# Turning the experts' inner rows in two row tiles of 64 tokens, in a decoder stack on one NeuronCore

## Chip, cores and metric

The kernel runs on one NeuronCore of a Trainium2 chip. The time is device microseconds of one execution; a figure for a kernel is the median of several runs. Engines: PE is TensorE's matmul, PEld its weight load, DVE VectorE, ACT ScalarE, POOL GpSimd, SP the engine that issues the weight transfers.

## What is computed

Two decoder blocks on 256 tokens of width 1024, all in fp32, end in a mixture of experts, in which this change lies. Cut to that part:

```python
def swiglu(h, wg, wu, wd):
    return (jax.nn.silu(h @ wg) * (h @ wu)) @ wd

def moe_swiglu(h, router, wg, wu, wd):          # 8 experts, top 2, inner width 3584
    t = h.reshape(B * S, D)
    logits = t.astype(jnp.float32) @ router.astype(jnp.float32)
    top_v, top_i = lax.top_k(logits, TOP_K)
    top_w = jax.nn.softmax(top_v, axis=-1)
    gates = jnp.sum(jax.nn.one_hot(top_i, N_EXPERTS, dtype=jnp.float32) * top_w[..., None], axis=1)
    out = jnp.zeros_like(t)
    for e in range(N_EXPERTS):
        out = out + gates[:, e:e + 1].astype(t.dtype) * swiglu(t, wg[e], wu[e], wd[e])
    return out.reshape(B, S, D)
```

The products keep fp32 accuracy. Most of them are three matmuls of operands that were split into a high part and a low part (`mm3`, L567 to L569: high by high, low by high, high by low); some take fp32 as it is.

## The kernel before

The program first runs the dense layers (to about 880 us), then routes the tokens, and then `mixture` computes the experts. The eight experts are sorted by how many tokens chose them. The five fullest (j below 5, "wide" here) get places for 128 tokens, the three emptiest (j from 5 on, "narrow") places for 64. Tokens beyond the places go through a second pass, `experts(Again)`, behind a flag; it does not run with these inputs.

**Chunks.** An expert's inner width of 3584 is cut into 7 chunks of 512 columns. The list `order` gives the 56 chunks, 35 wide and 21 narrow, in the order B B B F B B F B B F B B F B F B B F B B F B F B B F B B F B F B B F B B F B F B B F B B F B F B B F B B F B F F, where B is wide and F narrow. Each chunk c reads 6 weight slabs of 1 MB: two for the gate rows, two for the up rows, two for the way down.

**One turn of the loop over c on PE** is written out by hand:

1. the gate rows of chunk c (`rows_by`, two slabs): 24 matmuls of 512 columns for a wide chunk (L567 to L569), 32 records of L1233 for a narrow one. A narrow matmul uses 64 columns of the array, with its two halves side by side, and takes fp32 as it is;
2. `turn_hidden(c - 1)`: the inner rows `hh` of the chunk before, 128 places by 512 numbers, are transposed on PE by L1212 (`e.transpose`, a matmul of 128 rows with the unit matrix in `cb`) into one PSUM bank. There are 4 transposes of 128 by 128 for a wide chunk and 2 for a narrow one, whose 64 places by 512 lie as 128 by 256;
3. the up rows of chunk c, as in 1;
4. the way down of chunk c - 1 (`down_by`, two slabs), which has the turned rows as its stationary operand: L567 to L569 with `hTH` and `hTL` (wide), L1266 with `hTS` (narrow);
5. now and then gathers of later tokens (L1168, L1181) or the scatter of a finished expert back to its tokens (L1195, L1196 wide; L1203 narrow, a matmul on 64 rows of the array, its two halves on rows 0 to 63 and 64 to 127, into two banks).

The turn of c - 1 stands between two sets of rows of chunk c. What surrounds it is therefore told by the kind of c, and how long it is by the kind of c - 1. The turns of chunks 0 to 54 stand so; that of 55 stands between the two slabs of chunk 54's way down, which is narrow.

**Banks.** Banks 0 to 2 hold the sums of the way down. Banks 3 to 7 are handed out in a ring (`Ring.take`) to gate rows, up rows, turns, gathers and scatters. `claim` makes PE wait until the bank's last reader is through.

**The other engines.** ACT (`hi_to`, L1461) rounds each wide slab of 128 by 2048 to its high part `splitH`, and DVE (`lo_to`, L2161) subtracts for the low part `splitL`, two slabs ahead of PE, into three buffers each. Between these ACT copies the turned rows out of the bank (`turned_hidden`, L1461 again: to `hTH` for a wide chunk, to `hTS` for a narrow one) and DVE subtracts for `hTL` (L2879, wide alone). ACT also takes silu of the gate rows (L1986), and DVE multiplies it with the up rows into `hh` (L2912). SP issues each slab's transfer as soon as its buffer is free. The semaphores of a turn are `S.h` (rows ready), `S.h_turn` (turned), `S.ht_hi` (copied by ACT) and `S.ht_lo` (low part by DVE).

Of the kernel before, what the change touches and what calls it, by code (L numbers as in the profile page):

```python
# [7 lines left out]
F = mybir.dt.float32  # L8
# [143 lines left out]
def program(nc, x, mem, consts, w, out, cap):  # L152
    ctx = ExitStack()
    with ctx:
# [347 lines left out]

        class Again:

            jobs, c0, lo0, pair0, scat0, add0, y0 = 3, 56, 35, 3, 32, 32, 10
            chunks = [(j, i) for j in range(3) for i in range(7)]
            pairs = [[0, 1], [2]]

# [23 lines left out]
        INV = 1.0 / 384  # L532
        CW = PCOL["conv_w"]
        mid_order = {(q, m): 2 * q + m for q in range(2) for m in range(2)}

        def pcol(name, i):
            c = PCOL[name] + i
# [16 lines left out]
        def tensor(e):  # L554
# [579 lines left out]
            def mixture():  # L1134
# [69 lines left out]
                                 start=True, stop=True).then_inc(S.scat, 1)  # L1204

                def turn_hidden(q):
                    j = order[q][0]
                    b = bank["h", q] = ring.take()
                    t.wait_ge(S.h, q + 1)
                    o = claim(b, (S.ht_lo, many[q] + 1) if j < 5 else (S.ht_hi, q + 1))  # L1210
                    for k in range(4 if j < 5 else 2):
                        mm = e.transpose(o[:, 128 * k:128 * k + 128], every_other(hh[q % 2], k), ident)  # L1212
                    mm.then_inc(S.h_turn, 1)

                def rows_by(n, o, j, s):

# [20 lines left out]
                def down_by(n, q, s):  # L1237

                    j, i = order[q]
                    if j < 5:  # L1240
                        H, Lo = pieces(n)
                        turns = [(k, half) for k in range(2) for half in range(2)]
                        if (i, s) == (6, 1):
                            turns = [(k, half) for half in range(2) for k in range(2)]
                        t.wait_ge(S.lo, cut(n))
                        t.wait_ge(S.ht_lo, many[q] + 1)
                        if (i, s) == (0, 0):
                            for half in range(2):
                                claim(half, (S.ye_lo, 2 * j + half + 1))
                        for k, half in turns:  # L1250
                            kk = 2 * s + k
                            mm = mm3(banks[half][:, :], hTH[q % 2][:, 128 * kk:128 * kk + 128],
                                     hTL[q % 2][:, 128 * kk:128 * kk + 128], H[:, k, 512 * half:512 * half + 512],
                                     Lo[:, k, 512 * half:512 * half + 512], (i, s, k) == (0, 0, 0),
                                     (i, s, k) == (6, 1, 1))
                            if (k, half) == turns[-1] or ((i, s) == (6, 1) and (k, half) == turns[1]):
                                mm.then_inc(S.prod, 1)
                    else:
                        V = whole(n)
                        t.wait_ge(landed[home[n]], filled[n])  # L1260
                        t.wait_ge(S.ht_hi, q + 1)
                        if (i, s) == (0, 0):
                            claim(2, (S.ys, j - 4))
                        for k in range(2):
                            for half in range(2):
                                mm = e.matmul(banks[2][64 * half:64 * half + 64, :],  # L1266
                                              hTS[q % 2][:, 128 * k + 64 * s:128 * k + 64 * s + 64],
                                              V[:, k, 512 * half:512 * half + 512], start=(i, s, k) == (0, 0, 0),
                                              stop=(i, s, k) == (6, 1, 1))
                        mm.then_inc(S.prod, 1)  # L1270
# [180 lines left out]
        def scalar(e):  # L1451
# [468 lines left out]
            def mixture():  # L1920
# [33 lines left out]
                                   gcol[:, k:k + 1])  # L1954

                def turned_hidden(q):
                    a.wait_ge(S.h_turn, q + 1)
                    if q > 1:
                        a.wait_ge(S.prod, prod(slab_of(q - 2, 5)))
                    if order[q][0] < 5:  # L1960
                        copy(hTH[q % 2][:, :], banks[bank["h", q]][:, :]).then_inc(S.ht_hi, 1)
                    else:
                        copy(hTS[q % 2][:, :], banks[bank["h", q]][:, 0:256]).then_inc(S.ht_hi, 1)

                for n in range(4):
                    evict(0, n)
# [63 lines left out]
            def experts(B):  # L2030
# [14 lines left out]
                                       gcol[:, k:k + 1])  # L2045

                def turned_hidden(q):
                    a.wait_ge(S.h_turn, B.c0 + q + 1)
                    if q > 1:
                        a.wait_ge(S.prod, prod(B.slab(q - 2, 5)))  # L2050
                    copy(hTH[q % 2][:, :], banks[bank["h again", q]][:, :]).then_inc(S.ht_hi, 1)
# [84 lines left out]
        def vector(e):  # L2136
# [699 lines left out]
            def mixture():  # L2836
# [38 lines left out]

                def turned_hidden(q):
                    if order[q][0] < 5:
                        v.wait_ge(S.ht_hi, q + 1)
                        e.tensor_tensor(hTL[q % 2][:, :], banks[bank["h", q]][:, :], hTH[q % 2][:, :].bitcast(F),  # L2879
                                        ALU.subtract).then_inc(S.ht_lo, 1)  # L2880

                v.wait_ge(S.route, 4)
                v.wait_ge(S.in_rt, 32)
# [11 lines left out]
                for c in range(len(order) + 1):  # L2895
                    held = []
                    if c < len(order):
                        j, i = order[c]
                        width = 512 if j < 5 else 256
                        for s in range(2):  # L2900
                            lo_to(min(slab_of(c, s) + 2, main_end - 1))
                        if j >= 5:
                            lo_to(min(slab_of(c, 2) + 2, main_end - 1))
                        if c > 0:
                            turned_hidden(c - 1)
                        for s in range(2, 4):
                            lo_to(min(slab_of(c, s) + 2, main_end - 1))
                        v.wait_ge(S.silu, c + 1)
                        v.wait_ge(S.prod, prod(slab_of(c, 3)))
                        if c > 1:  # L2910
                            v.wait_ge(S.h_turn, c - 1)
                        e.tensor_tensor(hh[c % 2][:, 0:width], sg[c % 2][:, 0:width],  # L2912
                                        banks[bank["gu", c, 1]][:, 0:width], ALU.mult).then_inc(S.h, 1)
                        if c == 0:
                            pick(0, False)
                            pick_few(True)
                        if c == 3:
                            pick_few(False)
                        if j in (0, 2):
                            p = j // 2 + 1  # L2920
                            if i == 1:
                                pick(p, True)
                            if 2 <= i <= 5:
                                held.append((p, i - 2))
                            if i == 6:
                                pick(p, False)
                        if c == 7:
                            v.wait_ge(S.flag, 2)
                            flags["dve"] = e.value_load(flag[0:1, 0:1], min_val=0, max_val=1)
                    if c > 0:  # L2930
                        j, i = order[c - 1]
                        n = slab_of(c - 1, 5)
                        for s in range(2):
                            lo_to(min(n + 1 + s, main_end - 1))
                            for p, nn in held[:1 - s]:
                                evict(p, nn)
                            for j_, tb, half in back.get((c, s), ()):
                                v.wait_ge(S.scat, back_no[j_, tb, half])
                                add_block(j_, tb, half)
                            if s == 0 and c == len(order) - 1:  # L2940
                                turned_hidden(c)
                        if i == 6 and j < 5:
                            for half in range(2):
                                o = slice(512 * half, 512 * half + 512)
                                v.wait_ge(S.ye_hi, 2 * j + half + 1)
                                split_cols(S.ye_lo, yL[:, o], yH[:, o], banks[half][:, :])
# [6 lines left out]
            def experts(B):  # L2953
# [24 lines left out]
                                           ALU.add).then_inc(S.moe_add, 1)  # L2978

                def turned_hidden(q):  # L2980
                    v.wait_ge(S.ht_hi, B.c0 + q + 1)
                    e.tensor_tensor(hTL[q % 2][:, :], banks[bank["h again", q]][:, :], hTH[q % 2][:, :].bitcast(F),
                                    ALU.subtract).then_inc(S.ht_lo, 1)

# [4 lines left out]
                for c in range(len(B.chunks) + 1):  # L2989
                    evicted = None  # L2990
                    if c < len(B.chunks):
# [7 lines left out]
                        v.wait_ge(S.silu, B.c0 + c + 1)  # L2999
                        v.wait_ge(S.prod, prod(B.slab(c, 3)))  # L3000
                        if c > 1:
                            v.wait_ge(S.h_turn, B.c0 + c - 1)
                        e.tensor_tensor(hh[c % 2][:, :], sg[c % 2][:, :], banks[bank["gu again", c, 1]][:, :], ALU.mult)\
                            .then_inc(S.h, 1)
                        p = j // 2 + 1
# [268 lines left out]
```

## Time and profile before

| | us |
|---|---|
| runs | 1779.03 to 1779.14, median 1779.09 (3 runs) |
| the profiled execution, its own time | 1782.06 |
| its span (first to last instruction) | 1780.2 |
| PE busy | 1736.2 (98%) |
| DVE busy | 1186.6 (67%) |
| ACT busy | 915.4 (51%) |
| transfers from HBM | 492.36 MB |

Durations are from the one profiled execution. A row of the timeline gives the start of the first instruction in it, the time to the end of the last, engine, line, operation, output and inputs, shape and count. The shape begins with the rows and columns of the array that are in use: 128\*64 is a matmul on 128 rows and 64 columns, 64\*128 one on 64 rows. Durations of PE and PEld overlap, since matmuls are pipelined; what one costs is read from start to start. "(x n)" or "xn" is the number of instructions. A wait names the one that waits, then the one waited for.

### The profile page before, as it was taken

What the parts mean: (1) busy time and instruction counts of PE and PEld (TensorE: products, weight loads), DVE (VectorE), ACT (ScalarE), POOL (GpSimd) and SP (SyncE); (2) the same over time, 40 slices, a digit from 0 to 9 for tenths busy, and PEclk for the clock granted to TensorE, in tenths of its full rate; (3) what the DMA queues carried; (4) which work ended last, traced back from release to release, by engine and by line L of the source; (5) the groups of instructions that cost most, each with busy time, mean ns of one, the idle gap of its engine ahead of it and who ended that gap; (6) DMA issues with size and microseconds to landing.
All of it is one profiled execution on the core that took longest, in us unless ns stands there. A gap on an engine that the chain in (4) does not pass through costs nothing.

```text
span 1780.2 us, 25131 instructions
## 1 busy us (share of the span) xinstructions
PE 1736.2 (98%) x10391; PEld 1426.0 (80%) x10391; DVE 1186.6 (67%) x1517; ACT 915.4 (51%) x992; POOL 55.5 (3%) x71
## 2 busy tenths in 40 slices
PE   7999998999999999999999999999999999999997
PEld 7988887899988899999787777777777777776774
DVE  5664666767689566569686677565765676675663
ACT  5345565555454434444475555554554555554542
POOL 0000000000060000032000000000000000000000
PEclk9999999999999999999999999999999999999999
DMA  9533442475544385555747999999999999999995
GB/s 319 165 95 120 142 166 95 151 259 183 175 140 143 117 256 169 186 144 193 278 167 310 390 394 394 422 420 421 414 369 386 422 407 418 414 403 415 418 418 227
DMA packets 157545, 495.13 MB, mean 278 GB/s; under 512 B 9609, under 2 KB 99439, under 8 KB 114415
## 3 DMA queue, kind: packets, MB, share of 16 engines
q1 hardware_dynamic: 152911, 489.04, 72.0%
q10 hardware_dynamic: 4512, 4.40, 0.9%
q8 instruction: 84, 1.38, 0.3%
q14 instruction: 38, 0.31, 0.0%
HBM read 492.36 MB, written 1.05 MB: 277 GB/s over the span
## 4 chain that ended last, share of the span: by engine, by line
PE 87%; DVE 8%; ACT 4%; issue 1%; DMA 0%; DVEq 0%; ACTq 0%
PE bank L567 22%; PE bank L569 22%; PE bank L568 22%; PE bank L1233 8%; PE bank L1266 4%; DVE splitL L2161 3%; ACT splitH L1461 2%; PE bank L1212 1%; DVE co L2617 1%; PE bank L1168 1%; PE bank L1027 1%; PE bank L596 1%; PE bank L710 1%; PE bank L733 1%; PE bank L1085 0%
## 5 line engine op out<-in xcount | busy, mean ns | idle before, releaser
L2161 DVE TENSOR_TENSOR splitL<-raw,splitH 128x2048 fp32r<-128x2048 f32 (+1 forms) x248 | 562.2, 2272 | 194.8 <-ACT splitH L1461 194.1
L1461 ACT ACTIVATE splitH<-raw 128x2048 fp32r<-128x2048 f32 (+2 forms) x250 | 470.3, 1890 | 181.2 <-PE bank L569 112.9
L567 PE MATMUL bank<-RAH,splitH 128*128 128x256 f32 x1088 | 313.4, 288 | 5.9 <-DVE RAL L2171 3.3
L568 PE MATMUL bank<-RAL,splitH 128*128 128x256 f32 x1088 | 309.4, 284 | 0.0
L569 PE MATMUL bank<-RAH,splitL 128*128 128x256 f32 x1088 | 309.3, 284 | 0.0
L567 PE MATMUL bank<-splitH,RBH 128*128 128x512 f32 x736 | 293.6, 399 | 3.0 <-DVE splitL L2161 3.0
L569 PE MATMUL bank<-splitH,RBL 128*128 128x512 f32 x736 | 287.8, 391 | 0.0
L568 PE MATMUL bank<-splitL,RBH 128*128 128x512 f32 x736 | 287.1, 390 | 0.0
L2161 DVE TENSOR_TENSOR splitL<-rawx,splitH 128x2048 fp32r<-128x2048 f32 x89 | 203.7, 2289 | 53.3 <-ACT splitH L1461 52.8
L567 PEld LDWEIGHTS bank<-RAH,splitH 128*128 128x128 f32 x1088 | 210.2, 193 | 10.5 <-DVE RAL L2171 4.5
L1461 ACT ACTIVATE splitH<-rawx 128x2048 fp32r<-128x2048 f32 x89 | 170.3, 1914 | 83.9 <-PE bank L569 66.3
L568 PEld LDWEIGHTS bank<-RAL,splitH 128*128 128x128 f32 x1088 | 210.4, 193 | 1.1
L569 PEld LDWEIGHTS bank<-RAH,splitL 128*128 128x128 f32 x1088 | 210.2, 193 | 0.0
L567 PEld LDWEIGHTS bank<-splitH,RBH 128*128 128x128 f32 x736 | 138.6, 188 | 38.7 <-DVE splitL L2161 9.8
L569 PEld LDWEIGHTS bank<-splitH,RBL 128*128 128x128 f32 x736 | 138.3, 188 | 30.0
L568 PEld LDWEIGHTS bank<-splitL,RBH 128*128 128x128 f32 x736 | 138.6, 188 | 26.5
L567 PE MATMUL bank<-splitH,hTH 128*128 128x512 f32 x280 | 112.7, 403 | 0.0
L569 PE MATMUL bank<-splitH,hTL 128*128 128x512 f32 x280 | 109.3, 390 | 0.0
L568 PE MATMUL bank<-splitL,hTH 128*128 128x512 f32 x280 | 109.2, 390 | 0.0
L1233 PE MATMUL bank<-raw,xgS 128*64 128x256 f32 x864 | 100.5, 383 | 0.0
L2912 DVE TENSOR_TENSOR hh<-sg,bank 128x512 f32<-128x512 f32 (+1 forms) x56 | 32.7, 583 | 85.6 <-PE bank L569 71.1
L1233 PEld LDWEIGHTS bank<-raw,xgS 128*64 128x64 f32 x864 | 59.1, 137 | 33.7 <-issue 4.9
(340 smaller groups left out, 2171.3 us busy)
## 6 DMA issues: line engine op xcount, KB each, us to landing
raw<-in_moe_wg SPq DMA_DIRECT2D x71, 1024.0 KB, 8.6
raw<-in_moe_wd SPq DMA_DIRECT2D x69, 1024.0 KB, 9.8
raw<-in_moe_wu SPq DMA_DIRECT2D x68, 1024.0 KB, 10.0
rawx<-in_moe_wu SPq DMA_DIRECT2D x44, 1024.0 KB, 9.2
rawx<-in_moe_wd SPq DMA_DIRECT2D x43, 1024.0 KB, 10.2
rawx<-in_moe_wg SPq DMA_DIRECT2D x41, 1024.0 KB, 10.5
raw<-in_w_in SPq DMA_DIRECT2D x24, 1024.0 KB, 5.5
raw<-in_w_up SPq DMA_DIRECT2D x22, 1024.0 KB, 5.1
```

Of the source, the lines that this page charges most:

```text
L567: e.matmul(o, lh, rh, start=start, stop=False)
L568: e.matmul(o, lh, rl, start=False, stop=False)
L569: return e.matmul(o, ll, rh, start=False, stop=stop)
L596: mm = e.transpose(o[:, tb * 128:tb * 128 + 128], src[:, tb, k * 128:(k + 1) * 128], ident)
L710: mm = e.matmul(o[c][:, x0:x0 + wide], qA[p0:p0 + 64, h // 2, tb * 128:tb * 128 + 128], kA[p0:p0 + 64, h // 2, 0:wide], start=True, stop=True)
L733: mm = e.matmul(o[(j % 2) * 64:(j % 2) * 64 + 64, tb * 128:tb * 128 + 128], vA[:, sb, h * 64:(h + 1) * 64], PT[q % 2][:, x0 * 128:(x0 + 1) ...
L1027: mm = e.matmul(o[:, 0:256], diag[:, k, :], hc[:, 0, 2 + k:258 + k], start=(k == 0), stop=(k == 30))
L1233: mm = e.matmul(o[64 * h:64 * h + 64, 0:256], xgS[:, kk, 64 * (j - 5):64 * (j - 4)], V[:, k, 256 * h:256 * h + 256], start=kk == 0, stop=k ...
L1266: mm = e.matmul(banks[2][64 * half:64 * half + 64, :], hTS[q % 2][:, 128 * k + 64 * s:128 * k + 64 * s + 64], V[:, k, 512 * half:512 * hal ...
L1461: return e.activation(o, src, ACT.Copy)
L2161: e.tensor_tensor(l[:, 0:size], raws[home[n]][:, 0:size], h[:, 0:size].bitcast(F), ALU.subtract)\
L2912: e.tensor_tensor(hh[c % 2][:, 0:width], sg[c % 2][:, 0:width], banks[bank["gu", c, 1]][:, 0:width], ALU.mult).then_inc(S.h, 1)
```

## The change

In `mixture` (the second pass keeps its way of turning, and only its semaphore counts are shifted), a turn is made in halves of 64 rows:

- PE takes two banks from the ring, not one. Each 128 by 128 transpose becomes two of 64 by 128: one on the array's rows 0 to 63 into the first bank, one on rows 64 to 127 into the second, one after the other in turns. The moving operand is a quarter of the unit matrix with 64 columns. `S.h_turn` is raised twice.
- ACT copies each half by an instruction of its own, 64 columns of each block of 128, and raises `S.ht_hi` twice.
- DVE subtracts each half by itself and raises `S.ht_lo` twice.
- The waits count two for one. Nothing else is moved.

```diff
+        def by_halves(o, b, half):
+            n = o.shape[1] // 128
+            o = o[:, :].rearrange("p (k h t) -> p h k t", k=n, h=2)[:, half, :, :]
+            return o, None if b is None else b[:, 0:64 * n].rearrange("p (k t) -> p k t", k=n)
...
                 def turn_hidden(q):
                     j = order[q][0]
-                    b = bank["h", q] = ring.take()
+                    b = bank["h", q] = [ring.take(), ring.take()]
                     t.wait_ge(S.h, q + 1)
-                    o = claim(b, (S.ht_lo, many[q] + 1) if j < 5 else (S.ht_hi, q + 1))
-                    for k in range(4 if j < 5 else 2):
-                        mm = e.transpose(o[:, 128 * k:128 * k + 128], every_other(hh[q % 2], k), ident)
-                    mm.then_inc(S.h_turn, 1)
+                    o = [claim(b[half], (S.ht_lo, 2 * many[q] + half + 1) if j < 5 else (S.ht_hi, 2 * q + half + 1))
+                         for half in range(2)]
+                    last = 3 if j < 5 else 1
+                    for k in range(last + 1):
+                        for half in range(2):
+                            r = slice(64 * half, 64 * half + 64)
+                            mm = e.transpose(o[half][:, 64 * k:64 * k + 64], every_other(hh[q % 2], k)[r, :],
+                                             ident[r, r])
+                            if k == last:
+                                mm.then_inc(S.h_turn, 1)
...
                 def turned_hidden(q):
-                    a.wait_ge(S.h_turn, q + 1)
                     if q > 1:
                         a.wait_ge(S.prod, prod(slab_of(q - 2, 5)))
-                    if order[q][0] < 5:
-                        copy(hTH[q % 2][:, :], banks[bank["h", q]][:, :]).then_inc(S.ht_hi, 1)
-                    else:
-                        copy(hTS[q % 2][:, :], banks[bank["h", q]][:, 0:256]).then_inc(S.ht_hi, 1)
+                    for half in range(2):
+                        a.wait_ge(S.h_turn, 2 * q + half + 1)
+                        o, src = by_halves((hTH if order[q][0] < 5 else hTS)[q % 2], banks[bank["h", q][half]], half)
+                        copy(o, src).then_inc(S.ht_hi, 1)
...
                 def turned_hidden(q):
                     if order[q][0] < 5:
-                        v.wait_ge(S.ht_hi, q + 1)
-                        e.tensor_tensor(hTL[q % 2][:, :], banks[bank["h", q]][:, :], hTH[q % 2][:, :].bitcast(F),
-                                        ALU.subtract).then_inc(S.ht_lo, 1)
+                        for half in range(2):
+                            v.wait_ge(S.ht_hi, 2 * q + half + 1)
+                            o, src = by_halves(hTL[q % 2], banks[bank["h", q][half]], half)
+                            e.tensor_tensor(o, src, by_halves(hTH[q % 2], None, half)[0].bitcast(F), ALU.subtract)\
+                                .then_inc(S.ht_lo, 1)
```

The instructions of the changed kernel have line numbers 7 to 15 higher at these places. How the order changes is seen on PE at two places. The first is the turn of chunk 7 (wide) inside chunk 8 (wide); before:

```order
L568 MATMUL bank6<-splitL2_54,RBH_69 128x512
L569 MATMUL bank6<-splitH2_51,RBL_70 128x512
L1212 MATMUL bank7<-cb_71,hh1_157 128x128 x4
L567 MATMUL bank3<-splitH0_49,RBH_69 128x512
L568 MATMUL bank3<-splitL0_52,RBH_69 128x512
```

and now (the pair of banks 4 and 5 comes four times in all):

```order
L575 MATMUL bank3<-splitL2_54,RBH_69 128x512
L576 MATMUL bank3<-splitH2_51,RBL_70 128x512
L1224 MATMUL bank4<-cb_71,hh1_157 128x64
L1224 MATMUL bank5<-cb_71,hh1_157 128x64
...
L574 MATMUL bank6<-splitH0_49,RBH_69 128x512
L575 MATMUL bank6<-splitL0_52,RBH_69 128x512
```

Four transposes into one bank have become eight into two banks, with matmuls on all 128 rows on both sides of them as before. The second place is the turn of chunk 8 (wide) inside chunk 9 (narrow); before:

```order
L1233 MATMUL bank4<-raw3_58,xgS_161 64x256 x8
L1233 MATMUL bank4<-raw4_59,xgS_161 64x256 x8
L1212 MATMUL bank5<-cb_71,hh0_156 128x128 x4
L1233 MATMUL bank6<-raw1_56,xgS_161 64x256 x8
L1233 MATMUL bank6<-rawx2_169,xgS_161 64x256 x8
```

and now (again four pairs in all):

```order
L1247 MATMUL bank7<-raw3_58,xgS_161 64x256 x8
L1247 MATMUL bank7<-raw4_59,xgS_161 64x256 x8
L1224 MATMUL bank3<-cb_71,hh0_156 128x64
L1224 MATMUL bank4<-cb_71,hh0_156 128x64
...
L1247 MATMUL bank5<-raw1_56,xgS_161 64x256 x8
L1247 MATMUL bank5<-rawx2_169,xgS_161 64x256 x8
```

The neighbours here are matmuls on 64 columns of the array, and every bank number has moved on in the ring. On ACT and DVE the copies and low parts stay at their places, each as two instructions.

## Rows read from the trace of the kernel before

**Rows 1.** The page, part 1: engine, busy us (share), instructions.
```profile
PE 1736.2 (98%) x10391; PEld 1426.0 (80%) x10391; DVE 1186.6 (67%) x1517; ACT 915.4 (51%) x992; POOL 55.5 (3%) x71
```

**Rows 2.** Chain of waits by line, 900 us to the end.
```profile
by line: PE bank L567 22.0%; PE bank L569 21.2%; PE bank L568 21.1%; PE bank L1233 17.1%; PE bank L1266 8.2%; PE bank L1212 2.8%; PE bank L1168 1.6%; DVE splitL L2161 1.0%; PE bank L1195 0.8%; PE bank L1203 0.7%; PE bank L1181 0.6%; PE bank
```

**Rows 3.** Busy us and instructions by engine, 1000 to 1700 us; clock, DMA share, GB/s.
```profile
1000.00:1700.00 700.00, 699.76 (x3643) 508.91 (x3640) 460.03 (x310) 377.02 (x296) 0.00 (x0) 1.00 1.00 407
```

**Rows 4.** Waits, 905 to 1780 us: who <- whom: total us, times, longest.
```profile
ACT hTH L1461 <- PE bank L1212: 97.5, 35, 6.8
...
PE bank L567 <- DVE splitL L2161: 2.5, 3, 1.5
```

**Rows 5.** Timeline of PE (start, duration in us): four turns between wide rows.
```profile
1033.11 0.40 PE L569 MATMUL bank<-splitH,RBL 128*128 128x512 f32 x1
...
1033.34 0.63 PE L1212 MATMUL bank<-cb,hh 128*128 128x128 f32 x4
...
1033.69 0.28 PE L1212 MATMUL bank<-cb,hh 128*128 128x128 f32 x1
...
1034.04 0.39 PE L568 MATMUL bank<-splitL,RBH 128*128 128x512 f32 x1
```

**Rows 6.** Timeline of PE: two turns between wide rows.
```profile
1016.40 0.40 PE L569 MATMUL bank<-splitH,RBL 128*128 128x512 f32 x1
...
1017.10 0.39 PE L568 MATMUL bank<-splitL,RBH 128*128 128x512 f32 x1
```

**Rows 7.** Timeline of PE: four turns between narrow rows, the last also alone.
```profile
1001.01 0.39 PE L1233 MATMUL bank<-rawx,xgS 128*64 128x256 f32 x2
1001.33 0.75 PE L1212 MATMUL bank<-cb,hh 128*128 128x128 f32 x4
1002.00 0.44 PE L1233 MATMUL bank<-raw,xgS 128*64 128x256 f32 x2
...
1001.79 0.28 PE L1212 MATMUL bank<-cb,hh 128*128 128x128 f32 x1
```

**Rows 8.** Timeline of PE: matmuls on 64 rows between wide ones.
```profile
1535.30 0.39 PE L569 MATMUL bank<-splitH,hTL 128*128 128x512 f32 x1
...
1535.62 1.13 PE L1203 MATMUL bank<-ys,PtS 64*128 64x512 f32 x4
...
1536.15 0.60 PE L1203 MATMUL bank<-ys,PtS 64*128 64x512 f32 x2
...
1537.01 0.39 PE L568 MATMUL bank<-splitL,hTH 128*128 128x512 f32 x1
```

**Rows 9.** Timeline of PEld, the same place: second pair of loads, load after the last.
```profile
1535.72 0.19 PEld L1203 LDWEIGHTS bank<-ys,PtS 64*128 64x128 f32 x2
...
1536.67 0.19 PEld L567 LDWEIGHTS bank<-splitH,hTH 128*128 128x128 f32 x1 [0.76 <-issue]
```

**Rows 10.** Groups of ACT and DVE, 905 to 1770 us: busy, mean ns | idle before.
```profile
L1461 ACT ACTIVATE hTH<-bank 128x512 fp32r<-128x512 f32 x35 | 21.0, 599 | 97.5 <-PE bank L1212 97.5
...
L1461 ACT ACTIVATE hTS<-bank 128x256 f32<-128x256 f32 x21 | 8.1, 386 | 27.3 <-PE bank L1212 27.3
...
L1497 ACT ACTIVATE RBH<-bank,rr 128x128 fp32r<-128x128 f32 x24 | 7.5, 369 | 23.3 <-PE bank L1168 23.3
...
L2879 DVE TENSOR_TENSOR hTL<-bank,hTH 128x512 fp32r<-128x512 f32 x35 | 24.1, 687 | 42.7 <-ACT hTH L1461 42.7
...
L2912 DVE TENSOR_TENSOR hh<-sg,bank 128x256 f32<-128x256 f32 x21 | 8.7, 415 | 6.4 <-PE bank L1233 6.4
```

**Rows 11.** Timeline of PE: the wide row behind the first turns.
```profile
913.00 0.50 PE L567 MATMUL bank<-splitH,RBH 128*128 128x512 f32 x1 [1.47 <-DVE splitL L2161]
```

**Rows 12.** Timeline of DVE and PE: a low part and the wide row that reads it.
```profile
1146.63 2.28 DVE L2161 TENSOR_TENSOR splitL<-raw,splitH 128x2048 fp32r<-128x2048 f32 x1
...
1149.44 0.50 PE L567 MATMUL bank<-splitH,RBH 128*128 128x512 f32 x1
```

More of the change, by code:

```diff
@@ L503, in program @@
         class Again:
-            jobs, c0, lo0, pair0, scat0, add0, y0 = 3, 56, 35, 3, 32, 32, 10
+            jobs, c0, turn0, lo0, pair0, scat0, add0, y0 = 3, 56, 112, 70, 3, 32, 32, 10
             chunks = [(j, i) for j in range(3) for i in range(7)]
@@ L1245, in down_by @@
                         t.wait_ge(S.lo, cut(n))
-                        t.wait_ge(S.ht_lo, many[q] + 1)
+                        t.wait_ge(S.ht_lo, 2 * many[q] + 2)
                         if (i, s) == (0, 0):
@@ L1260, in down_by @@
                         t.wait_ge(landed[home[n]], filled[n])
-                        t.wait_ge(S.ht_hi, q + 1)
+                        t.wait_ge(S.ht_hi, 2 * q + 2)
                         if (i, s) == (0, 0):
@@ L2047, in turned_hidden @@
                 def turned_hidden(q):
-                    a.wait_ge(S.h_turn, B.c0 + q + 1)
+                    a.wait_ge(S.h_turn, B.turn0 + q + 1)
                     if q > 1:
@@ L2910, in mixture @@
                         if c > 1:
-                            v.wait_ge(S.h_turn, c - 1)
+                            v.wait_ge(S.h_turn, 2 * (c - 1))
                         e.tensor_tensor(hh[c % 2][:, 0:width], sg[c % 2][:, 0:width],
@@ L2980, in turned_hidden @@
                 def turned_hidden(q):
-                    v.wait_ge(S.ht_hi, B.c0 + q + 1)
+                    v.wait_ge(S.ht_hi, B.turn0 + q + 1)
                     e.tensor_tensor(hTL[q % 2][:, :], banks[bank["h again", q]][:, :], hTH[q % 2][:, :].bitcast(F),
@@ L3001, in experts @@
                         if c > 1:
-                            v.wait_ge(S.h_turn, B.c0 + c - 1)
+                            v.wait_ge(S.h_turn, B.turn0 + c - 1)
                         e.tensor_tensor(hh[c % 2][:, :], sg[c % 2][:, :], banks[bank["gu again", c, 1]][:, :], ALU.mult)\
```

## The prediction

> **What bounds the kernel now.** I read the page's first part, then the chain of waits of the mixture, then its busy times by stretch, then single turns in the timeline. PE is busy for 98% of the span [rows 1], and from 900 us on the chain of waits is almost wholly PE's own lines: L567 to L569 make 64% of it, the narrow L1233 and L1266 another 25%, the turns L1212 2.8% [rows 2]. From 1000 to 1700 us PE stands still for 0.24 us in all, at the full granted clock, while DVE is busy for 460 and ACT for 377 of 700 us [rows 3]. Its matmuls wait for a low part three times, 2.5 us together [rows 4]. So one microsecond more or less of PE's stream in the mixture is nearly one more or less of the time. The change touches that stream in 56 places, the turns, and I ask what a turn costs between its neighbours. The copies wait for the turns, 97.5 us in 35 waits [rows 4], and PE does not wait for the copies: the way down that reads them stands behind the up rows, 24 matmuls of 0.23 us for a wide chunk.
>
> **How the turns stand.** By the order of chunks 34 turns lie between wide rows (15 of them of a wide chunk, with 4 transposes, and 19 of a narrow one, with 2) and 22 between narrow rows (20 with 4, 2 with 2).
>
> **A turn between wide rows, before.** From the start of the last L569 to the start of the first L568 behind the turn it is 1034.04 - 1033.11 = 0.93 us with four transposes [rows 5], and 1017.10 - 1016.40 = 0.70 with two [rows 6]. Nothing else stands between but one L567. The transposes go without a pause: the first starts 0.23 us behind the L569, as any next matmul does, and the fourth 0.35 behind the first, so one takes 0.12 [rows 5].
>
> **The same, after.** The matmuls now use half of the array's rows. The trace of before has such ones, L1203, two halves in two banks, set between wide matmuls [rows 8]. Three things are read there. Going in: the first starts 0.32 us behind the L569, not 0.23, and its weights are loaded only then, where those of a transpose were loaded under the matmul before. Within: the second pair of loads starts 0.10 behind the first [rows 9], and four records of 512 columns fit in two steps of 0.53 us, so the two halves do load and run side by side. But a pair still takes about as long to load as one transpose takes now; I take 0.11 for each. Going out: the L567 behind is loaded only once the last half is through, and L568 starts 1537.01 - 1536.67 = 0.34 behind that load [rows 8, 9]. How soon the load may follow comes from a turn between narrow rows: 0.21 us behind the start of the last transpose [rows 7]. It streams 64 columns now instead of 128, half of its 0.12, so I take 0.15. The sum for four pairs is 0.32 + 4 x 0.11 + 0.15 + 0.34 = 1.25, against 0.93: 0.32 more. For two pairs it is 0.32 + 0.22 + 0.15 + 0.34 = 1.03 against 0.70: 0.33 more. What the shorter transposes give back is small, since the loads, not the columns, set their pace.
>
> The bounds of this price: below, no pause at all at either end, which leaves the turn shorter by the 0.06 of its last stream and the 0.02 that rounding hides, 0.08 less; above, the whole 0.52 us from the last pair of L1203 to the next load (1536.67 - 1536.15, [rows 8, 9]) in place of 0.15, 0.70 more. That row has 512 columns to stream and a transpose has 64, so I stay with the row of a transpose.
>
> The Trainium skill speaks on both sides. TensorEngine Tiling (Array Packing), Key Properties, says that a change of the tiling mode, not just of the tile, drains TensorE; the pauses of 0.32 and 0.34 us agree. TensorE: Matmul & The Clock Gate, LDWEIGHTS, says that a load takes its time by the columns and not by the contract dimension; its rule of columns through 1.2 GHz gives an estimate of 0.107 us for 128 columns, and the sum would be the same by it.
>
> **A turn between narrow rows.** These matmuls use 64 columns of the array, so PE changes its mode at both ends already. Before, it is 1002.00 - 1001.01 = 0.99 us from the last pair of L1233 to the next pair, with four transposes [rows 7]. After: 0.32 to the first load (1001.33 - 1001.01), 4 x 0.11, and 0.15 = 0.91, that is 0.08 less. Two transposes: about 0.07 less.
>
> **The sum on PE.** Of the 34 turns between wide rows one costs nothing: behind that of chunk 0 PE waits 1.47 us for a low part anyway [rows 11]. 14 x 0.32 + 19 x 0.33 = 10.8 us more; 20 x 0.08 + 2 x 0.07 = 1.7 us less. Net 9.1 us more.
>
> **Copies and low parts in halves.** ACT's copy of 128x512 takes 0.60 us; two of 256 columns by the row of `hTS` are 2 x 0.39, so 0.18 more. For a narrow chunk 0.39 becomes two of 128 columns, at most 2 x 0.37 by the row of that size, 0.35 more. DVE's 0.69 becomes 2 x 0.42 by the row of `hh`, 0.15 more [rows 10]. All this stands ahead of a `splitH` on ACT or a `splitL` on DVE, for which PE may wait. What hides it is the lead of the low parts: even one that was held up by DVE's product for `hh` ended at 1146.63 + 2.28 = 1148.91, 0.53 us before PE's row at 1149.44 [rows 12], and the added 0.35 fits in. Cost nought; with that cover gone at every wide turn at most 35 x 0.18 = 6 us, and the ACT and DVE parts overlap since DVE may start on the first half. An earlier `hTL` gains nothing either, as PE does not wait for it. The extra increments of semaphores go with the matmuls.
>
> **The second bank.** Each turn waits for one bank more, and every bank comes round sooner. With five in the ring the added one was mostly used last by the turn before or by up rows whose product PE awaits anyway for `S.h`. Nothing. SP's transfers are issued when slabs are used up: with PE slower they come later, and the full DMA engines [rows 3] get relief.
>
> On its own time the profiled execution would go from 1782.06 to 1791.2 us. It stands 3.0 us above the median of the runs shown; the sum carries over to the median: 1779.1 + 9.1 = **1788.2 us**. A measurement of this kernel tells about 0.2%, 3.6 us, from no change.
>
> **Rivals.**
>
> - *Half the time for a turn, pauses paid.* Two row tiles work side by side, so four pairs of 64 columns might take 4 x 0.06 us and not 4 x 0.11. That gives back 0.20 on each of the 34 other wide-chunk turns and 0.10 on each of 21, 8.9 us in all, and the time is 1779.3, the same as before. For it: the halves of L1203 do run together. Against it: its loads of 64 rows follow each other at 0.10. Chance 0.06. (The Trainium skill has this as a rule, TensorEngine Tiling (Array Packing), Theoretical Speedup: up to 2x where a dimension is 64 or less. The rows of L1203 show it for 512 columns; no row shows it for 64.)
> - *No pauses: faster.* If the pauses at L1203 came from its waits for `ys`, and not from its mode, turns would slip in as before: 55 x 0.08 = 4.4 us less, 1774.7; with the halved pairs as well 13.3 less, 1765.8. It decides once the two pauses together fall under the 0.08 us saved. Against it: the same 0.32 stands in front of the transposes between narrow rows, which wait for nothing new. Chance 0.11 for both together, of which a third is the deeper one.
> - *The halves load one after the other.* Then a pair takes 0.22, 0.11 more for each of 4 x 34 + 2 x 21 = 178 pairs: 19.6 us on top, 1807.8. Against it: the row at 0.10. For it: transposes might pair differently from matmuls. Chance 0.07.
> - *ACT and DVE late.* The 6 us above on top of the sum: 1794. Chance 0.04.
>
> **Numbers.** My forecast has 0.72: inside it from 1784 to 1792, for 0.02 to 0.05 either way in each price. The range takes in the case without gain and that of late copies, 1778 to 1795; left out are the faster cases and the serial loads, 0.18. The upper bound of the price, 33 x 0.37 = 12 us on top, would end at 1800 and is left out too, since its row streams eight times the columns. Faster by over 0.2%: 0.11. Within: 0.06, and 0.02 for the low end of the forecast. Slower: 0.81.
>
> **What would show it.** In the changed profile, a turn between wide rows lasts 1.25 us from L576 to L575 with four pairs, and 1.03 with two; the weight load stands idle for some 0.3 us ahead of it and again behind; a turn between narrow rows takes 0.9. The pairs start 0.11 apart. PE's busy time hides the pauses in part, so the starts must be read. The waits of L574 to L576 for `splitL` stay near three, and ACT's copies number 112. I am wrong if the L574 behind a turn loads under the last pair, if pairs start 0.06 or 0.22 apart, or if PE's idle time grows by waits for `splitL` or for a bank.

## The result

| | before | after |
|---|---|---|
| median | 1779.14 us (5 runs, 1779.03 to 1780.60) | 1789.65 us (5 runs, 1788.33 to 1790.05) |
| the profiled execution, its own time | 1782.06 | 1788.33 |
| its span | 1780.2 | 1786.4 |

The ratio after to before is 1.0051, with a 95% interval of 1.0040 to 1.0062: the change makes the kernel 9.1 us slower, between 7.1 and 11.0. The medians alone differ by 10.5. The forecast was 1788.2, which is 9.1 more.

The two profiled executions differ by only 6.2 us of span, which misleads. The first turn starts at 910.90 us in the one of before and at 908.09 in the one of after, so 2.8 us of the difference were made ahead of the mixture, where the program is the same. From the first turn to the end of the span it is 1780.2 - 910.9 = 869.3 us in the one and 1786.4 - 908.1 = 878.3 in the other, 9.0 more. Below I compare turns, and this stretch, not spans.

First the page of after, part 1, and the busy times of 1000 to 1700 us, as in [rows 1, 3]:

```profile
PE 1741.2 (97%) x10573; PEld 1421.9 (80%) x10573; DVE 1187.7 (66%) x1552; ACT 918.9 (51%) x1048; POOL 55.9 (3%) x71
...
1000.00:1700.00 700.00, 699.76 (x3742) 503.07 (x3741) 458.21 (x335) 375.75 (x338) 0.00 (x0) 1.00 0.99 404
```

PE is as full as before by this view, at the full granted clock. That is because a matmul's recorded time reaches beyond its turn on the array and covers the pauses: a wide matmul is recorded for 0.39 us, and the next one starts 0.23 behind it. The weight load's busy time shows more: 503 us in this stretch instead of 509, with 101 loads more. The pauses are seen in the starts. The timeline of PE in after, at the turn of chunk 7 between wide rows, with its last pair alone, then the first wide matmul of the next way down, answers to [rows 5]:

```profile
1031.41 0.39 PE L576 MATMUL bank<-splitH,RBL 128*128 128x512 f32 x1
1031.72 0.69 PE L1224 MATMUL bank<-cb,hh 64*128 64x64 f32 x8
...
1032.13 0.29 PE L1224 MATMUL bank<-cb,hh 64*128 64x64 f32 x2
...
1032.35 0.50 PE L574 MATMUL bank<-splitH,RBH 128*128 128x512 f32 x1
1032.69 0.39 PE L575 MATMUL bank<-splitL,RBH 128*128 128x512 f32 x1
...
1037.90 0.39 PE L574 MATMUL bank<-splitH,hTH 128*128 128x512 f32 x1
```

And the timeline of its weight loads, with the idle time before them in brackets:

```profile
1031.72 0.56 PEld L1224 LDWEIGHTS bank<-cb,hh 64*128 64x128 f32 x8 [0.35 <-issue]
1032.35 0.19 PEld L574 LDWEIGHTS bank<-splitH,RBH 128*128 128x128 f32 x1
1032.46 0.19 PEld L575 LDWEIGHTS bank<-splitL,RBH 128*128 128x128 f32 x1
```

From L576 to L575 it is 1032.69 - 1031.41 = 1.28 us, where it was 0.93. The first load comes 0.31 us behind L576, after 0.35 us of an idle load unit. The load of L574 comes 0.22 behind the last pair and L575 another 0.34 behind that. Held against [rows 5], the way in is 0.08 longer (0.31 for 0.23), the way from the first transpose to the last 0.06 (0.41 for 0.35), and the way from the last one to the wide matmul L575 0.21 (0.56 for 0.35). Over half of the loss lies behind the turn. The other two kinds, in the timeline of PE (two turns between wide rows, then four between narrow rows, the last pair of these also alone), answer to [rows 6, 7]:

```profile
1014.40 0.39 PE L576 MATMUL bank<-splitH,RBL 128*128 128x512 f32 x1
1014.72 0.45 PE L1224 MATMUL bank<-cb,hh 64*128 64x64 f32 x4
1015.10 0.50 PE L574 MATMUL bank<-splitH,RBH 128*128 128x512 f32 x1
1015.44 0.39 PE L575 MATMUL bank<-splitL,RBH 128*128 128x512 f32 x1
...
1046.72 0.39 PE L1247 MATMUL bank<-raw,xgS 128*64 128x256 f32 x2
1047.04 0.69 PE L1224 MATMUL bank<-cb,hh 64*128 64x64 f32 x8
...
1047.44 0.28 PE L1224 MATMUL bank<-cb,hh 64*128 64x64 f32 x2
...
1047.66 0.44 PE L1247 MATMUL bank<-raw,xgS 128*64 128x256 f32 x2
```

Two turns between wide rows take 1.04 us instead of 0.70, four between narrow rows 0.94 instead of 0.99. All turns of a kind agree within 0.01, but for that of chunk 0, behind which PE waits anyway.

The copies and waits in after (groups of ACT and DVE, then waits: total us, times, longest) answer to [rows 4, 10]:

```profile
L1475 ACT ACTIVATE hTH<-bank 128x256 fp32r<-128x256 f32 x70 | 23.1, 381 | 105.3 <-PE bank L1224 105.3
L1475 ACT ACTIVATE hTS<-bank 128x128 f32<-128x128 f32 x42 | 9.4, 276 | 30.3 <-PE bank L1224 30.3
...
L2894 DVE TENSOR_TENSOR hTL<-bank,hTH 128x256 fp32r<-128x256 f32 x70 | 26.3, 417 | 44.5 <-ACT hTH L1475 44.5
```

```profile
PE bank L574 <- DVE splitL L2174: 2.5, 3, 1.4
```

PE waits for low parts three times and 2.5 us, exactly as before. Halving the copies added 2.1 us to ACT for `hTH`, 1.3 for `hTS`, and 2.2 to DVE, all of it hidden.

### The profile page after: what moved, and what is told of

Its sections match the earlier page's. It is cut to its first block, busy times and chain, and to the rows that moved or that the text cites. A ratio compares the mean times of both kernels' runs of the same rounds, so it can differ in the third digit from the quotient of the medians.

```text
span 1786.4 us, 25583 instructions
## 1 busy us (share of the span) xinstructions
PE 1741.2 (97%) x10573; PEld 1421.9 (80%) x10573; DVE 1187.7 (66%) x1552; ACT 918.9 (51%) x1048; POOL 55.9 (3%) x71
## 3 DMA queue, kind: packets, MB, share of 16 engines
q8 instruction: 85, 1.39, 0.3%
## 4 chain that ended last, share of the span: by engine, by line
PE 86%; DVE 8%; ACT 4%; issue 1%; DMA 0%; DVEq 0%; ACTq 0%
PE bank L574 22%; PE bank L576 21%; PE bank L575 21%; PE bank L1247 8%; PE bank L1280 4%; DVE splitL L2174 3%; ACT splitH L1475 2%; PE bank L1224 2%; DVE co L2630 1%; PE bank L1175 1%; PE bank L1034 1%; PE bank L603 1%; PE bank L717 1%; PE bank L740 1%; PE bank L1092 0%
## 5 line engine op out<-in xcount | busy, mean ns | idle before, releaser
L574 PE MATMUL bank<-RAH,splitH 128*128 128x256 f32 x1088 | 311.7, 287 | 7.0 <-DVE RAL L2184 3.3
L576 PE MATMUL bank<-RAH,splitL 128*128 128x256 f32 x1088 | 307.7, 283 | 0.0
L575 PE MATMUL bank<-RAL,splitH 128*128 128x256 f32 x1088 | 307.7, 283 | 0.0
L574 PE MATMUL bank<-splitH,RBH 128*128 128x512 f32 x736 | 293.4, 399 | 3.0 <-DVE splitL L2174 3.0
L575 PE MATMUL bank<-splitL,RBH 128*128 128x512 f32 x736 | 286.9, 390 | 0.0
L576 PE MATMUL bank<-splitH,RBL 128*128 128x512 f32 x736 | 286.6, 389 | 0.0
L574 PEld LDWEIGHTS bank<-RAH,splitH 128*128 128x128 f32 x1088 | 208.4, 192 | 11.7 <-DVE RAL L2184 4.5
L575 PEld LDWEIGHTS bank<-RAL,splitH 128*128 128x128 f32 x1088 | 208.5, 192 | 1.0
L576 PEld LDWEIGHTS bank<-RAH,splitL 128*128 128x128 f32 x1088 | 208.5, 192 | 0.0
L574 PEld LDWEIGHTS bank<-splitH,RBH 128*128 128x128 f32 x736 | 138.2, 188 | 40.3 <-DVE splitL L2174 8.0
L576 PEld LDWEIGHTS bank<-splitH,RBL 128*128 128x128 f32 x736 | 138.2, 188 | 29.4
L575 PEld LDWEIGHTS bank<-splitL,RBH 128*128 128x128 f32 x736 | 138.4, 188 | 26.0
L574 PE MATMUL bank<-splitH,hTH 128*128 128x512 f32 x280 | 112.7, 403 | 0.0
L576 PE MATMUL bank<-splitH,hTL 128*128 128x512 f32 x280 | 109.3, 390 | 0.0
L575 PE MATMUL bank<-splitL,hTH 128*128 128x512 f32 x280 | 109.1, 390 | 0.0
```

Of the source, the lines that this page charges most:

```text
L574: e.matmul(o, lh, rh, start=start, stop=False)
L575: e.matmul(o, lh, rl, start=False, stop=False)
L576: return e.matmul(o, ll, rh, start=False, stop=stop)
```

## The experiments

In each, the two theories are: **the mode**, that PE pauses when it changes between using all its rows and half of them, and that a pair costs one load of 128 columns; and, as rivals, **the rest** (second bank, halved copies), **the halves one after the other**, and **the halves at their 64 columns' pace**.

### Two banks and halved copies alone

```diff
+                    if not rows_apart(q):
+                        for k in range(last + 1):
+                            half, at = divmod(2 * k, last + 1)
+                            at = 64 * at
+                            mm = e.transpose(o[half][:, at:at + 128], every_other(hh[q % 2], k), ident)
+                            if k in (last // 2, last):
+                                mm.then_inc(S.h_turn, 1)
+                        return
```

`rows_apart` is false for every turn here. ACT and DVE copy the matching half of the blocks from each bank, in the same number of instructions and elements as in the change.

> Two banks, two copies and two low parts per turn as in the change, but the transposes stay on all 128 rows (the first half of the blocks into one bank, the second half into the other). If the mode of the array costs the time: as before, 1779 us within 2, turns between wide rows 0.94 and 0.70 us as before. If the second bank or the late copies cost it: near 1789.

Measured: 1780.71 us against 1779.34 before, ratio 1.0002 (0.9993 to 1.0011). The timeline of PE there, at the turn of chunk 7:

```profile
1032.02 0.40 PE L581 MATMUL bank<-splitH,RBL 128*128 128x512 f32 x1
1032.25 0.63 PE L1230 MATMUL bank<-cb,hh 128*128 128x128 f32 x4
1032.64 0.47 PE L579 MATMUL bank<-splitH,RBH 128*128 128x512 f32 x1
1032.95 0.39 PE L580 MATMUL bank<-splitL,RBH 128*128 128x512 f32 x1
```

0.93 us from L581 to L580, as before. The second bank, the second copy and the second low part cost at most 2 us by the interval. The trace is finer: from the first turn to the end it is 1779.1 - 909.7 = 869.4 us, against 869.3 before. The loss is in the row tiles.

### Row tiles only between wide rows, and only between narrow rows

```diff
+        def rows_apart(q):
+            return not (q == 55 or order[q + 1][0] > 4)
```

This is the one with row tiles between wide rows; the other has the same condition without `not`. All other turns are made as in the kernel above.

> Row tiles only in the 34 turns between wide rows; the 22 others on all 128 rows. Pauses at the change of mode: 33 x 0.34 = 11.2 us more than before, 1790.3, slightly more than the change itself. If a turn costs the same everywhere: 34/56 of 10.5, 6.4 more.

> Row tiles only in the 22 turns between narrow rows. Pauses at the change of mode: 22 x 0.05 = 1.1 us less than before, about 1778. If a turn costs the same everywhere: 22/56 of 10.5, 4.1 more, 1783.

Measured: between wide rows alone 1789.96 us, ratio 1.0054 (1.0038 to 1.0069); between narrow rows alone 1779.62, ratio 0.9996 (0.9986 to 1.0005), both against 1779.34. The place decides: 34 turns carry the loss, and the other 22 carry none of it. That those 22 gain is below what the times can tell, but the trace has it, with 0.93 us for a four-block turn between narrow rows in place of 0.99. From the first turn to the end it is 879.2 us with row tiles between wide rows and 868.3 with row tiles between narrow rows, 9.9 more and 1.0 less than before; together that is the 9.0 of the change but for 0.1.

### One more transpose, of 128 or of 64 rows

```diff
                     for k in range(4 if j < 5 else 2):
-                        mm = e.transpose(o[:, 128 * k:128 * k + 128], every_other(hh[q % 2], k), ident)
+                        e.transpose(o[:, 128 * k:128 * k + 128], every_other(hh[q % 2], k), ident)
+                    mm = e.transpose(o[:, 0:128], every_other(hh[q % 2], 0), ident)
```

The other kernel has `o[:, 0:64], every_other(hh[q % 2], 0)[0:64, :], ident[0:64, 0:64]` in the added line.

> The kernel before with one redundant transpose on all 128 rows at the end of each turn (it repeats the first). 55 x 0.12 = 6.6 us more than before, 1785.9, by every theory.

> The kernel before with one redundant transpose of 64 rows at the end of each turn. If PE pauses at each change of mode, the load of the 64 rows waits for the transposes and the load behind waits for it: 0.46 us more between wide rows and 0.26 between narrow rows, 33 x 0.46 + 22 x 0.26 = 20.9, 1800. If the small transpose costs only its own load: 55 x 0.11 = 6, about 1785.

Measured against 1780.33: 1787.08 us, ratio 1.0037 (1.0023 to 1.0051), for 128 rows; 1800.13, ratio 1.0113 (1.0096 to 1.0130), for 64 rows. One small transpose in each turn costs 19.8 us and one large one 6.8, about a third of it. The timeline of PE with the 64-row one, between wide and between narrow rows:

```profile
1032.22 0.40 PE L569 MATMUL bank<-splitH,RBL 128*128 128x512 f32 x1
1032.46 0.63 PE L1212 MATMUL bank<-cb,hh 128*128 128x128 f32 x4
1033.02 0.33 PE L1213 MATMUL bank<-cb,hh 64*128 64x64 f32 x1
1033.28 0.50 PE L567 MATMUL bank<-splitH,RBH 128*128 128x512 f32 x1
1033.61 0.39 PE L568 MATMUL bank<-splitL,RBH 128*128 128x512 f32 x1
...
1047.67 0.39 PE L1234 MATMUL bank<-raw,xgS 128*64 128x256 f32 x2
1047.99 0.74 PE L1212 MATMUL bank<-cb,hh 128*128 128x128 f32 x4
1048.66 0.33 PE L1213 MATMUL bank<-cb,hh 64*128 64x64 f32 x1
1048.92 0.44 PE L1234 MATMUL bank<-raw,xgS 128*64 128x256 f32 x2
```

From L569 to L568 it is 1.39 us, 0.46 over [rows 5]; from pair to pair of L1234 it is 1.25, 0.26 over [rows 7]. It needs neither a second bank, a second copy, nor a pair to lose that time: a single instruction on half the rows between others on all rows is enough. A 128-row transpose more costs 0.12 at either place, by the trace of the kernel that adds it. Over that, the small one costs 0.46 - 0.12 = 0.34 between wide rows, where it brings two changes of mode that were not there, and 0.26 - 0.12 = 0.14 between narrow rows, where two changes become three. So the loss follows the number of changes, at 0.14 to 0.17 us each, and the change of mode is shown as the cause.

### The pairs twice, and both halves on the same rows

```diff
-                    for k in range(last + 1):
+                    for step in range(2 * last + 2):
+                        k = step % (last + 1)
...
-                            if k == last:
+                            if step == 2 * last + 1:
```

```diff
-                            r = slice(64 * half, 64 * half + 64)
+                            r = slice(0, 64)
```

> The change with each turn's pairs issued twice over. 182 pairs more, no mode change more. If a pair costs its load of 128 columns, 0.11 each, 20 us more than the change, 1809.7. If it costs its 64 columns alone, 0.06 each, 11 more, 1800.6. If the halves load one after the other, 0.22 each, 40 more.

> The change with both halves taken from rows 0 to 63, into the two banks, so that the inner rows of places 64 to 127 are left out and those of 0 to 63 used twice. If the two row tiles work side by side in the change, here they can't: one more load of 0.11 us for each of 178 pairs, 19 us more than the change, 1808.8. If they never did: as the change, 1789.7.

Measured against 1780.33: the pairs twice 1809.82 us, ratio 1.0168 (1.0151 to 1.0185); one tile 1810.26, the same ratio and interval. Against after, both are 20 to 21 us more. The turn of chunk 7 in the timeline of PE, first with the pairs twice:

```profile
1034.04 0.39 PE L576 MATMUL bank<-splitH,RBL 128*128 128x512 f32 x1
1034.36 1.17 PE L1225 MATMUL bank<-cb,hh 64*128 64x64 f32 x16
1035.46 0.50 PE L574 MATMUL bank<-splitH,RBH 128*128 128x512 f32 x1
1035.80 0.39 PE L575 MATMUL bank<-splitL,RBH 128*128 128x512 f32 x1
```

and then with one tile:

```profile
1034.00 0.39 PE L576 MATMUL bank<-splitH,RBL 128*128 128x512 f32 x1
1034.32 1.17 PE L1224 MATMUL bank<-cb,hh 64*128 64x64 f32 x8
1035.42 0.50 PE L574 MATMUL bank<-splitH,RBH 128*128 128x512 f32 x1
1035.75 0.39 PE L575 MATMUL bank<-splitL,RBH 128*128 128x512 f32 x1
```

Sixteen small transposes in two tiles fill the same 1.17 us as eight in one. So the two tiles do work side by side in the change, and each pair costs 0.12 us: (1.76 - 1.28) / 4. That is what one transpose of 128 rows costs [rows 5], though a pair has 64 columns to stream and not 128. Row tiles halve the work per instruction, double the instructions, run them two at a time, and end where they began. Both rivals about the pace of the pairs are ruled out.

### Fewer changes of mode: the turn ahead of the narrow rows

```diff
                         j, i = order[c]
+                        early = c > 1 and j > 4 and order[c - 2][0] < 5
+                        if early:
+                            turn_hidden(c - 1)
...
-                            if which == 0 and c > 0:
+                            if which == 0 and c > 0 and not early:
                                 turn_hidden(c - 1)
```

> The kernel before, with the turn of 15 chunks moved from between the narrow gate and up rows of the next chunk to ahead of its gate rows, behind a wide way down, so that PE changes its mode once less on each side. By the mode: 0.77 - 0.47 = 0.30 us less each, 4.5 less, 1774.6. If the pauses go with the transposes and not with the mode: no change. If the inner rows are not ready in time: slower, with waits of L1212 for hh.

Measured: 1775.38 us (9 runs) against 1779.34 (25 runs), ratio 0.9972 (0.9962 to 0.9982), which is 5.0 us less, between 3.2 and 6.8. The timeline of PE there, at the turn of chunk 8, which stood between narrow rows before:

```profile
1042.21 0.40 PE L569 MATMUL bank<-splitH,hTL 128*128 128x512 f32 x1
1042.45 0.63 PE L1212 MATMUL bank<-cb,hh 128*128 128x128 f32 x4
1043.01 1.30 PE L1233 MATMUL bank<-raw,xgS 128*64 128x256 f32 x10
```

The first transpose follows the wide matmul at 0.24 us, without a pause. The one change of mode that is left, to the narrow rows, was there before too; the two around the turn are gone. In the trace, 14 of the 15 places that the turns left are 0.78 us shorter and 14 of the 15 that they went to 0.47 to 0.48 longer (0.54 and 0.24 for the one turn of two transposes); 0.05 more is saved in the narrow rows behind. That makes 0.34 to 0.35 for each, 5.2 in all, and from the first turn to the end it is 864.2 us, 5.1 less than before. Nothing waits for `hh`: it is ready by then. This version is faster than both kernels, and it comes from reading the same rows the other way: not to make the turn smaller, but to put it where PE is in its mode already.

## Why the prediction was right

**The bound.** It was PE's stream, as said. The waits for low parts did not grow, and halved copies and the second bank alone change nothing.

**The turn between wide rows.** The forecast was 0.32 us more with four pairs and 0.33 with two; measured are 0.34 and 0.34. The way in was right (0.31 and 0.32 against 0.32). Two terms were off, in opposite directions. The way out was put at 0.15, since the last transpose streams half as many columns; measured is 0.22, no less than the 0.21 of a transpose with 128 columns [rows 7]. The pairs were put at 4 x 0.11 = 0.44 to the start of the last; measured is 1032.13 - 1031.72 = 0.41. The first starts with its load, the second 0.17 behind the first, and the others 0.12 apart. One sign did not come as said: the load unit was to stand idle for some 0.3 us behind the turn too. It does ahead of the turn, 0.35, but behind it only for 1032.35 - 1032.28 = 0.07 by its records; the pause there shows in the starts alone.

**The turn between narrow rows.** The forecast was 0.08 us less, measured 0.05 less, and the reason given for most of it failed. Of the saving 0.06 was to come from the last transpose's shorter stream, but the way out takes 0.21 us as before. What became shorter is the way from the first transpose to the last, 0.41 us over the 20 turns of this kind instead of 0.46 [rows 7]: behind the change of mode a row-tiled pair is followed by the next at 0.17, where a transpose on all rows was at 0.22. That this term came out on the forecast's side is luck.

**The count.** Of the 56 turns one was put in the wrong class. That of chunk 55 stands behind a wide scatter, not between narrow matmuls. In the timeline of PE of before, then of after:

```profile
1759.16 0.39 PE L1196 MATMUL bank<-yL,Pt 128*128 128x512 f32 x1
1759.39 0.39 PE L1212 MATMUL bank<-cb,hh 128*128 128x128 f32 x2
1759.71 1.08 PE L1266 MATMUL bank<-raw,hTS 128*64 128x512 f32 x4
```

```profile
1765.18 0.40 PE L1203 MATMUL bank<-yL,Pt 128*128 128x512 f32 x1
1765.51 0.45 PE L1224 MATMUL bank<-cb,hh 64*128 64x64 f32 x4
1765.89 1.08 PE L1280 MATMUL bank<-raw,hTS 128*64 128x512 f32 x4
```

It lasts 0.71 instead of 0.55 us, 0.16 more and not 0.07 less. The turn of chunk 0 was absorbed by the wait behind it, but for 0.08 us (2.75 instead of 2.67 from the last L569 to the first L568). With two banks and halved copies alone it is 2.75 as well, so these 0.08 are not of the row tiles.

**The sum.** 33 x 0.34 - 21 x 0.05 + 0.16 + 0.08 = 10.4 us at the turns, against 9.1 forecast. Part of it comes back (below), 1.3 us, and 9.1 remain. That this is the forecast to the tenth is luck: the interval of the measurement is 4 us wide.

**Copies.** For narrow chunks I had bounded the added time by 0.35 us per turn; it is 2 x 0.28 - 0.39 = 0.17. It was hidden either way.

**Rivals.** That turns take half the time and that nothing pauses are both refuted, as is that the halves load one after the other. That ACT and DVE come too late is refuted by the waits, three and 2.5 us as before. Two tiles do work side by side: a pair takes 0.12 us in two tiles and twice that in one. That gains nothing here, where the blocks were 128 rows deep and the full array had no idle rows to start with. The Trainium skill, TensorEngine Tiling (Array Packing), Theoretical Speedup, gives up to 2x where a dimension is 64 or less. For the pairs, counted by instructions, the trace agrees.

## What to carry to other kernels

A matmul on half of the array's rows, between others on all of them, costs some 0.34 us here for the two changes, with one small transpose in it as with two or four pairs; so short work in another tiling goes next to work of the same tiling, and cutting a full 128-row transpose in two row tiles saves nothing to set against it. In a stream that a full engine bounds, count such changes in the instruction order and look for a place that does without: moving 15 turns by one step gained 5 us here. Judge by starts in the timeline, since busy time covers pauses of this size.

## What was not expected

**The way out has a floor.** The load behind a transpose in another mode starts 0.21 to 0.22 us after the transpose's start, with 64 columns in row tiles as with 128 on all rows. That the shorter stream would show was my mistake; which part of the transpose sets this floor stays open.

**Wide matmuls run closer together behind a row-tiled turn.** From the turn's last wide matmul to the first of the next way down it is 1039.29 - 1033.11 = 6.18 us before (the timeline of PE has the latter as below) and 1037.90 - 1031.41 = 6.49 after. That is 0.31 more, though the turn itself took 0.35 more.

```profile
1039.29 0.39 PE L567 MATMUL bank<-splitH,hTH 128*128 128x512 f32 x1
```

The 22 steps behind a turn take 5.027 us on average over 33 turns before and 4.987 after: 0.04 us for each turn, 1.3 in all. With two banks and halved copies alone, or with row tiles between narrow rows alone, they take 5.03; with row tiles between wide rows alone 4.99. So it goes with the row-tiled turn and not with the copies. With both halves on the same rows, or with the lone transpose of 64 rows, they take 5.01 to 5.02 us, in between. Why the matmuls behind a turn on all rows are a little farther apart was not tried.
